# Third mixer of a two-block transformer: where the compression products stand between the projections

## What is computed

```python
def mixer_c(x, w_in, gate_b, cmp_pos, cmp_w1, cmp_w2, w_out, rel_bias):
    p = jnp.einsum('bsd,de->bse', x, w_in)
    q = p[..., :1024] ...
    kv = p[..., C_OFF_KV:C_OFF_GATE].reshape(Bn, S, 3, 2, G, E)
    gates = jax.nn.sigmoid(p[..., C_OFF_GATE:] + gate_b)
    def compress(t, pos, w1, w2):
        blocks = t[:, cidx] + pos[None, None, :, None, :]
        flat = blocks.transpose(0, 3, 1, 2, 4).reshape(Bn, G, n_cmp, CMP_BLOCK * E)
        return jax.nn.gelu(flat @ w1) @ w2
    k_cmp = compress(kv[:, :, 0, 0], cmp_pos[0], cmp_w1[0], cmp_w2[0])
    v_cmp = compress(kv[:, :, 0, 1], cmp_pos[1], cmp_w1[1], cmp_w2[1])
    ...
    # three attention branches per head: compressed, selected, window
    return jnp.einsum('bse,ed->bsd', g0 * o_c + g1 * o_s + g2 * o_w, w_out)
```

## Time and profile before

| | before |
|---|---|
| median of 3 runs | 2474.19 us (2473.15 to 2478.47) |
| the profiled execution, its own time | 2479.86 us |
| its span from first to last instruction | 2478.1 us |
| mean granted TensorE clock | 0.965 |
| busy: PE / DVE / ACT / POOL | 2356.3 / 1589.9 / 1010.6 / 81.4 us |
| mixer `c`, from the first product of c_in.1 to the first score on VectorE | 1930.90 to 1997.11 us |

### The profile page before, as it was taken

How to read it: one execution, slowest core, us unless ns; L and a number is a source line. 1 busy time by engine, 2 the same in 40 slices (tenths; PEclk the granted TensorE clock), 3 DMA queues, 4 the chain that set the end, 5 groups by cost and what they waited for, 6 DMA issues and landing times.

```text
span 2478.1 us, 41302 instructions
## 1 busy us (share of the span) xinstructions
PE 2356.3 (95%) x17730; PEld 2051.0 (83%) x17730; DVE 1589.9 (64%) x2291; ACT 1010.6 (41%) x1327; POOL 81.4 (3%) x116
## 2 busy tenths in 40 slices
PE   6999989999999998889999999999999979999997
PEld 6999749999999777787999988777787958777786
DVE  7887476876887636654755674533796465543795
ACT  3333254334333132342334552433674352433673
POOL 0000000000000002550000000000000000000000
PEclk8999989999999999999999998999999988999999
DMA  8986304874777231001754530867993520877991
GB/s 332 356 314 250 127 26 159 300 286 148 287 302 293 98 136 52 3 3 60 264 179 179 165 101 1 337 271 275 366 353 140 204 91 1 332 271 280 362 353 49
DMA packets 48429, 502.13 MB, mean 203 GB/s; under 512 B 4984, under 2 KB 9592, under 8 KB 11000
## 3 DMA queue, kind: packets, MB, share of 16 engines
q1 hardware_dynamic: 42624, 491.57, 52.2%
q10 hardware_dynamic: 5624, 7.93, 1.3%
HBM read 496.33 MB, written 3.15 MB: 202 GB/s over the span
## 4 chain that ended last, share of the span: by engine, by line
PE 78%; DVE 13%; DMA 4%; issue 3%; ACT 2%; POOL 1%; DVEq 0%; SPq 0%; ACTq 0%; POOLq 0%
PE PS L629 23%; PE PS L1273 21%; PE PS L699 7%; PE PS L675 5%; DMA ring<-stream 4%; PE PS L1284 2%; PE PS L576 2%; DVE work L1975 2%; PE PS L1300 1%; PE PS L1008 1%; PE PS L712 1%; PE PS L811 1%; DVE w_up_lo L2016 1%; DVE work L2188 1%; PE PS L1359 1%
## 5 line engine op out<-in xcount | busy, mean ns | idle before, releaser
L629 PE MATMUL PS<-x_part_hi,w_up_hi 128*128 128x256 f32 x1408 | 404.4, 287 | 11.4 <-DVE w_up_lo L2016 7.7
L629 PE MATMUL PS<-x_part_hi,w_up_lo 128*128 128x256 f32 x1408 | 398.4, 283 | 0.0
L629 PE MATMUL PS<-x_part_lo,w_up_hi 128*128 128x256 f32 x1408 | 398.4, 283 | 0.0
L2591 DVE TENSOR_TENSOR ring_low<-ring,m_w_up 128x2048 fp32r<-128x2048 f32 x96 | 219.6, 2291 | 144.6 <-ACT m_w_up L1814 144.6
L629 PEld LDWEIGHTS PS<-x_part_hi,w_up_hi 128*128 128x128 f32 x1408 | 269.8, 192 | 16.1 <-DVE w_up_lo L2016 10.1
L629 PEld LDWEIGHTS PS<-x_part_lo,w_up_hi 128*128 128x128 f32 x1408 | 270.2, 192 | 0.0
L629 PEld LDWEIGHTS PS<-x_part_hi,w_up_lo 128*128 128x128 f32 x1408 | 270.0, 192 | 0.0
L1814 ACT ACTIVATE m_w_up<-ring 128x2048 fp32r<-128x2048 f32 x96 | 183.9, 1916 | 150.9 <-PE PS L1273 137.1
L2016 DVE TENSOR_TENSOR w_up_lo<-ring,w_up_hi 128x2048 fp32r<-128x2048 f32 x88 | 201.2, 2289 | 20.0 <-ACT w_up_hi L1471 20.0
L1273 PE MATMUL PS<-ring_low,xg_hi 128*128 128x512 f32 x512 | 202.8, 396 | 0.0
L1273 PE MATMUL PS<-m_w_up,xg_lo 128*128 128x512 f32 x512 | 202.2, 395 | 0.0
(11 more groups left out here) (533 smaller groups left out, 4939.8 us busy)
## 6 DMA issues: line engine op xcount, KB each, us to landing
ring<-stream SPq DMA_DIRECT2D x133, 2048.0 KB, 7.9
ring<-stream SPq DMA_DIRECT2D x88, 1536.0 KB, 6.8
work<-stream SPq DMA_DIRECT2D x48, 1024.0 KB, 7.8
hT<-stream SPq DMA_DIRECT2D x16, 1024.0 KB, 9.1
ring<-stream SPq DMA_DIRECT2D x3, 1152.0 KB, 5.7
const<-const_tables ACTq DMA_DIRECT2D x1, 2207.0 KB, 12.4
bias_scratch<-work ACTq DMA_DIRECT2D x1, 2048.0 KB
work<-bias_scratch ACTq DMA_DIRECT2D x2, 1024.0 KB, 6.9
```

What stands on the lines that cost most here:

```text
L629: last = mm(out, w[a][:, lo:lo + P], x[b][:, at:at + T], start=start and i == 0, stop=stop and i == 2, skip_group_check=skip)
L2591: tt_(ring_low[n][:, part], ring[n][:, part], m_w_up[g % 3][:, :].bitcast(F32), ALU.subtract).then_inc(S("up_split"), 1)
```

## The change

The columns of `w_in` are packed in another order: c_in.0 is now the source of the compression, c_in.1 and c_in.2 are the queries, c_in.3 and c_in.4 keys and values as before. In the load list two compression pieces stand behind c_in.1, two behind c_in.2, and `cmp_w2` behind c_in.3. TensorE does the first two compression pieces behind c_in.1, the other two behind c_in.2, the sum over groups between the two halves of c_in.3, the second product ahead of c_in.4. ScalarE and VectorE follow this order, the results go to other PSUM banks (6, 7 for the compression, 0 to 3 for keys and values), and ScalarE's roundings keep their place ahead of the copies.

```diff
@@ stream_plan
-    p += c_in[:1] + [("c_gates", 8 * 24)] + c_in[1:]
-    p += [("cmp_w1.0", 4096), ("cmp_w1.1", 4096), ("cmp_w1.2", 4096), ("cmp_w1.3", 4096), ("cmp_w2", 512)]
+    cmp_w1 = cols("cmp_w1", [512] * 4)
+    p += c_in[:1] + [("c_gates", 8 * 24), c_in[1]] + cmp_w1[:2] + [c_in[2]] + cmp_w1[2:] + [c_in[3], ("cmp_w2", 512), c_in[4]]
@@ TensorE, c()
-                for i, b in ((3, 6), (4, 0)):
-                    pe.wait_ge(S("c_copied"), 2)
-                    g = HALF_AT[f"c_in.{i}"]
-                    half_tiles(g, mix_x, [2 * b, 2 * b + 1])
-                    half_tokens(g + 1, mix_x, lambda tt: bank(b + 1, T, tt * T))
-                pe.wait_ge(S("c_copied"), 5)
-                line.next("cmpb_ready")
-                for kv in range(2):
+                def compress(kv):
...
+                for i in range(3):
+                    split_piece(f"c_in.{i}", mix_x, range(4 * i, 4 * i + 4), passes=None if i else x_halves())
+                    if i == 0:
+                        take("c_gates")
+                        by_token("c_gates", 6, 0, 24, 24, 24, ("c_gate_b", 0)).then_inc(slot_free, 1)
+                    else:
+                        if i == 1:
+                            pe.wait_ge(S("c_copied"), 2)
+                            line.next("cmpb_ready")
+                        compress(i - 1)
+                pe.wait_ge(S("c_copied"), 1)
+                g = HALF_AT["c_in.3"]
+                half_tiles(g, mix_x, [0, 1])
+                pe.wait_ge(S("c_copied"), 4)
                 for kv in range(2):
                     line.next("cmp_raw")
...
                 last.then_inc(S("cmp_turned"), 1)
+                half_tokens(g + 1, mix_x, lambda tt: bank(1, T, tt * T))
                 take("cmp_w2")
...
                 last.then_inc(slot_free, 1)
+                g = HALF_AT["c_in.4"]
+                half_tiles(g, mix_x, [4, 5])
+                half_tokens(g + 1, mix_x, lambda tt: bank(3, T, tt * T))
                 pe.wait_ge(S("cmp_copied"), 1)
                 pe.wait_ge(S("c_copied"), 6)
                 attention("c")
@@ ScalarE, c()
-                for i, (dst, b) in enumerate(((W(C_Q, 1024), 0), (W(C_Q + 1024, 1024), 2), (W(C_SRC, 1024), 4))):
+                for i, (dst, b) in enumerate(((W(C_SRC, 1024), 0), (W(C_Q, 1024), 2), (W(C_Q + 1024, 1024), 4))):
                     mix_highs("c", 2 * i + 3, 2 * i + 4)
                     act.wait_ge(*used(f"c_in.{i}"))
...
-                mix_highs("c", 9)
-                for i, b in ((3, 6), (4, 0)):
-                    act.wait_ge(*used(f"c_in.{i}"))
-                    fn(W(C_KV + 512 * (i - 3), 512), bank(b), ACT.Copy)
-                    fn(W(C_KV + 1024 + 512 * (i - 3), 512), bank(b + 1), ACT.Copy).then_inc(S("c_copied"), 1)
...
-                mix_highs("c", 10)
+                mix_highs("c", 9)
                 act.wait_ge(slot_free, FREED["cmp_w2"])
...
+                for i, b in ((3, 0), (4, 2)):
+                    act.wait_ge(*used(f"c_in.{i}"))
+                    fn(W(C_KV + 512 * (i - 3), 512), bank(b), ACT.Copy)
+                    fn(W(C_KV + 1024 + 512 * (i - 3), 512), bank(b + 1), ACT.Copy).then_inc(S("c_copied"), 1)
+                    if i == 3:
+                        mix_highs("c", 10)
@@ VectorE, c()
-                mix_lows("c", 2, 3, 4, 5, 6, 7, 8)
-                dve.wait_ge(S("c_copied"), 4)
+                mix_lows("c", 2, 3, 4)
+                dve.wait_ge(S("c_copied"), 1)
...
-                mix_lows("c", 9)
+                mix_lows("c", 5, 6, 7, 8, 9)
                 dve.wait_ge(S("bias_in"), 64)
@@ packing of the weights
-    put_cols("c_in", w[:, :2560])
+    put_cols("c_in", np.concatenate([w[:, 1024:1536], w[:, :1024], w[:, 1536:2560]], 1))
```

More of the change, by code:

```diff
@@ L1406, in c @@
                             n = 32 if at + 32 <= 960 else 2 * NCMP
-                            last = mm(bank(4 + 2 * kv, T, T, lo, lo + n), b3[:, at:at + n],
+                            last = mm(bank(6 + kv, T, T, lo, lo + n), b3[:, at:at + n],
                                       piece(name)[:, i * T:(i + 1) * T], start=(half == 0 and i < 4),
@@ L1421, in c @@
                 for m in range(2):
-                    mm(bank(3, 2 * NCMP), w2[:, m, :], hid[:, m, :], start=(m == 0), stop=(m == 1))
+                    mm(bank(7, 2 * NCMP), w2[:, m, :], hid[:, m, :], start=(m == 0), stop=(m == 1))
                 for g in range(2):
                     for m in range(2):
-                        last = mm(bank(3, P, P + g * P, 0, NCMP), hid[:, 2 + m, g * NCMP:(g + 1) * NCMP], w2[:, 2 + m, :],
+                        last = mm(bank(7, P, P + g * P, 0, NCMP), hid[:, 2 + m, g * NCMP:(g + 1) * NCMP], w2[:, 2 + m, :],
                                   start=(m == 0), stop=(m == 1))
                 last.then_inc(slot_free, 1)
+                g = HALF_AT["c_in.4"]
+                half_tiles(g, mix_x, [4, 5])
+                half_tokens(g + 1, mix_x, lambda tt: bank(3, T, tt * T))
                 pe.wait_ge(S("cmp_copied"), 1)
@@ L1912, in c @@
                         fn(W(C_G, 48), bank(6, 48), ACT.Sigmoid).then_inc(S("c_copied"), 1)
-                mix_highs("c", 9)
-                for i, b in ((3, 6), (4, 0)):
-                    act.wait_ge(*used(f"c_in.{i}"))
-                    fn(W(C_KV + 512 * (i - 3), 512), bank(b), ACT.Copy)
-                    fn(W(C_KV + 1024 + 512 * (i - 3), 512), bank(b + 1), ACT.Copy).then_inc(S("c_copied"), 1)
                 for kv in range(2):
                     act.wait_ge(slot_free, FREED[f"cmp_w1.{2 * kv + 1}"])
-                    fn(W(C_RAW + kv * T, T), bank(4 + 2 * kv, T, T), ACT.Copy).then_inc(S("cmp_raw"), 1)
+                    fn(W(C_RAW + kv * T, T), bank(6 + kv, T, T), ACT.Copy).then_inc(S("cmp_raw"), 1)
                 act.wait_ge(S("cmp_turned"), 1)
@@ L1924, in c @@
                 last.then_inc(S("hid_gelu"), 1)
-                mix_highs("c", 10)
+                mix_highs("c", 9)
                 act.wait_ge(slot_free, FREED["cmp_w2"])
-                fn(W(C_KC, 30), bank(3, 30), ACT.Copy)
-                fn(W(C_VC, 256, 0, NCMP), bank(3, 256, P, 0, NCMP), ACT.Copy).then_inc(S("cmp_copied"), 1)
+                fn(W(C_KC, 30), bank(7, 30), ACT.Copy)
+                fn(W(C_VC, 256, 0, NCMP), bank(7, 256, P, 0, NCMP), ACT.Copy).then_inc(S("cmp_copied"), 1)
+                for i, b in ((3, 0), (4, 2)):
[4 more added lines that the diff above has]
+                        mix_highs("c", 10)
                 attention("c", {6: [lambda: mix_highs("c", 11)]})
```

## The result

Beside five runs of each, the change took 2488.31 us (median, 2481.95 to 2493.03) and the kernel before 2477.56 us (2473.15 to 2482.93). The ratio is 1.0037, with a 95% interval of 1.0020 to 1.0055: **slower**, by 5 to 14 us; that is under one per cent, but the interval lies clear of 1. Measured again later, with 12 runs (median 2486.77 us) beside 35 of the kernel before (median 2480.05 us, 2472.60 to 2487.51), the ratio is 1.0026 (1.0012 to 1.0040), or 6.4 us.

What follows compares the result with a forecast made beforehand. The prediction took a chain 78% TensorE and 13% VectorE as the bound. Terms up to the first score gave +5.0 us, with +1.8 for the clock and -1.25 for attention +5.5; 2474.19 + 5.5 = 2479.7 us, range 2475.3 to 2483.5.

Steps and rivals of the forecast that it cites:

- The step that failed: Carrying the difference from the profiled execution, 2479.86 us, to the runs' median, 5.7 us lower: 2474.19 + 5.5 = 2479.7 us.
- rival C: Clock low throughout: both compression pieces at half, attention no better, 3.6 us more at half; +10.3, 2484.5 us; chance 0.08.
- first two pieces: The first two compression pieces on TensorE, one at full and one at half clock: 5.4 us, bounds 3.6 and 7.2.
- half 7 with the clock's loss: Half 7 behind the small products: 5.67 us, plus 1.8 us for half clock after the wait, bounds 0 and 1.8.
- copies and subtraction at the end: Behind c_in.4's last product: copies 1.1 us, then VectorE's subtraction for half 10, 2.2 us, before the first score.
- First stall: Before the first compression product: ScalarE holds the source's copy behind half 4's rounding, waiting for c_in.2's load; TensorE stands 5.0 us.
- Second stall: Before half 6: c_in.3 lands 5.75 us behind cmp_w1.3, and its split takes 4.25 us; TensorE waits 1.1 us.
- Rival B: Loads come faster, 4.83 us behind another instead of 5.75, second stall vanishes: +2.6, 2476.8 us, nothing measurable; chance 0.11.
- Third stall: Before the raw results' products: ScalarE's copies stand behind half 8's rounding, which waits for c_in.4's load; TensorE waits 2.5 us.
- The second product: The product between half 7 and c_in.4, taken from the earlier timeline (1992.02 to 1994.06): 2.04 us.
- Attention: Behind the block: attention starts behind dense work, so less half clock; 1.25 us taken back, bounds 0 and 3.0.
- A: ScalarE is not held and the three stalls do not arise: -6.7, 2467.5 us, faster; chance 0.07.

Runs made afterwards that it cites:

- b1: The change with ScalarE copying the compression's source before half 4's rounding and VectorE adding positions before half 4's subtraction; block 67.7 us, whole 1.0000 against the kernel before.
- c1: The change with only its load list altered, c_in.2 loaded fourth again, ahead of the four compression pieces; block 75.7 us, whole 1.0033 against the kernel before.
- b2: The change with ScalarE copying c_in.2's result and the two raw results before half 8's rounding; block 66.9 us, whole 1.0005 against the kernel before.
- b3: The change with both ScalarE reorderings, those of b1 and b2; block 67.5 us, whole 0.9997 against the kernel before.
- e1: The change with VectorE's subtraction of half 10 moved ahead of its wait for the sixth c_copied count; block 71.0 us, whole 1.0017 against the kernel before.
- e2: The change with the edits of b2 and e1 together; block 66.1 us, whole 1.0004 against the kernel before.
- a0: The change run again without an edit; block 72.6 us, whole 1.0026 against the kernel before.
- v1: Another order than the change's: two compression pieces behind c_in.2, two behind c_in.4, loads and helper lists re-sorted; block 60.0 us, whole 0.9957 against the kernel before.
- v2: The kernel of v1 run again without an edit; block 59.9 us, whole 0.9977 against the kernel before.

## Why the prediction was right or wrong

The direction was right and so were two of the three stalls; the absolute time and its range were wrong: 2479.7 us with 2475.3 to 2483.5, against 2488.31 us. In microseconds against before the forecast was +5.5, the first comparison gave +9.2 (5 to 14), the second +6.4 (3.0 to 9.9).

**The step that failed** is the one that carried the difference to the median of the runs: "2474.19 + 5.5". The three runs behind 2474.19 covered 5 us. Thirty-five runs of the same kernel cover 15 us and have their median at 2480.05. I knew from the page that the profiled execution lay 5.7 us higher, took that as an offset, and gave the base no width at all; the range held only unknowns of the change. Against a base of 2480 the sum ends at 2485.5 us, 1 us from the 2486.77 us of the repeated measurement. Of the first comparison the base explains a part only. Its own base, the median of five, was 2477.56 us; from there the sum ends at 2483.1 us and its range at 2486.9, still under 2488.31. Of the 8.6 us missed, 3.4 are this base, and 5.2 are a difference of medians of 10.75 us where I had 5.5. That the same two kernels lay 6.7 us apart in the repeated measurement suggests that most of the 5.2 us is the scatter of five runs, and not an error of the sum. Besides, the prediction's "2475.7 to 2483.2" is printed without its working, and it is not what its bounds give: those add up to +0.1 and +8.6, and +10.3 is reached only with the extra 1.8 us of rival C.

Term by term, against the first trace of the change:

| term | forecast | measured |
|---|---|---|
| wait before the first compression product | 5.0 | 5.24 |
| first two pieces | 5.4 | 5.21 |
| c_in.2 | 11.34 | 11.56 (1959.18 to 1970.74) |
| last two pieces | 3.6 | 3.63 |
| wait before half 6 | 1.1 | 0 |
| wait before the raw sums | 2.5 | 3.34 |
| half 7 with the clock's loss | 5.67 + 1.8 | 7.27 (1984.52 to 1991.79) |
| second product | 2.04 | 1.43 (1991.79 to 1993.22) |
| c_in.4 | 11.34 | 11.71 (1993.22 to 2004.93) |
| copies and subtraction at the end | 3.3 | 3.4 (2004.93 to 2008.34) |
| block against before, ahead of attention | +6.8 | +6.47 |
| attention, first score to last | -1.25 | +0.2, and -0.9 in the repeated trace |

That +6.8 and +6.47 lie so close is in part luck: the wait before half 6 and the second product came out 1.7 us too high in the forecast, the wait before the raw sums and the projections c_in.2 and c_in.4 1.4 us too low.

*First stall*: right in place, cause and size; b1 and c1 show that it is half 4's place on ScalarE and c_in.2's place in the ring, for either edit removes it.

*Second stall*: wrong, and its size went into the third. I had loads land 5.75 us behind one another. The pair in the place of the earlier trace rows lands 5.9 us apart (issued 1931.52 and 1935.76, 7.8 and 9.5 us), but cmp_w1.3 and c_in.3 (issued 1957.58 and 1959.31) only 4.9:

```profile
ring<-stream SPq DMA_DIRECT2D x1, 2048.0 KB, 7.5
ring<-stream SPq DMA_DIRECT2D x1, 2048.0 KB, 10.7
```

The Trainium skill's page "DMA: Bandwidth & Descriptors", section "Anatomy of one DMA", gives its fit (2.0 us and the bytes at 436 GB/s) for DMAs issued by GpSimd, and these loads are issued by SyncE, which the prediction does not say. As an estimate for 2048 KB the fit makes 4.8 us behind another load and 6.8 us alone. Here one of the two pairs agrees with it (4.9 us) and the other does not (5.9 us), and a load alone took 7.6 us (c_in.4, issued 1972.74). Rival B was right about that one pair, not about the time, since TensorE, starting half 6 earlier, waited 0.8 us more behind it.

*Third stall and its clock*: right. b2 took the wait and the half clock out together, and the block fell by 5.7 us.

*The second product* was read from a stretch partly at half clock: the prediction has 1.00 everywhere but in the rows it names, yet the granted clock was 0.50 from 1993 us on. Behind dense work it took 1.4 us. A gain of 0.6 us missed.

*Attention*: in the change's first trace the gain taken back is not there, for the clock fell to 0.50 with the first score. The other traces speak for it. In b1, b2, b3, e1 and e2, whose attention stands behind the same dense work, the clock stayed at 1.00 for another 5 us, and attention took 50.9 to 52.3 us against the 52.9 of the one trace before; in a0 and c1 it fell at once, and attention took 52.0 and 52.1. Behind small products (v1, v2) it took 53.0. So the -1.25 us may be right on the average; one trace before can't decide it, and what makes the clock fall at once or later is open. The first score and two microseconds further, in the change and in b1 (columns as in the earlier trace rows):

```profile
2008.34:2010.34 2.00, 1.28 (x4) 0.97 (x5) 1.76 (x8) 0.75 (x5) 0.00 (x0) 0.52 0.00 0
2010.34:2012.34 2.00, 1.04 (x5) 0.93 (x4) 1.42 (x5) 1.21 (x5) 0.00 (x0) 0.50 0.00 0
```
```profile
2002.86:2004.86 2.00, 0.96 (x5) 0.56 (x5) 1.83 (x9) 0.75 (x5) 0.00 (x0) 1.00 0.00 0
2004.86:2006.86 2.00, 0.58 (x4) 0.48 (x4) 1.83 (x8) 1.75 (x8) 0.00 (x0) 1.00 0.00 0
```

*The rivals*: A would have needed c_in.2's landing by 1935.2; in the change it landed at 1945.3 with everything 4.8 us later, so within half a microsecond of the time foreseen. C, the clock low throughout, did not come. The measured range of the whole reaches up to C's +10.3, the block does not.

## What to carry to other kernels

In a strict list with a ring of load slots, moving a piece moves its load, and every instruction behind the first that waits for that load. Before laying work between tiles, write down for each load which slot it waits for and when it lands, and sort the helper engines' lists by those landings; the same idea, the compression between the projections, gained 6 us in the block or lost 6, by where it was put and how the loads and lists followed. And give the base of a prediction the width that repeated measurements of unchanged code have: single runs of the kernel before lay 15 us apart, and its medians, of 3 to 35 runs, between 2474.2 and 2480.3 us, as far apart as the effect.

## What the runs showed that I had not expected

Equal code reached the start of c_in.1 anywhere between 1927.5 and 1938.9 us in twelve traces, 11.4 us apart, and took 476.0 to 481.4 us behind the block. The granted clock goes with this behind the block: from the first score to the end it was 0.98 in the three traces with 476.0 us (b1, b2, e1), 0.97 in e2 with 478.2, and 0.96 in the eight others, with 478.2 to 481.4. Whether it makes all of the scatter, and what decides how often it falls in equal code, I did not find out. Inside the block of the change's two traces it does not vary so: the stretch at half clock around the first compression pieces stands at the same place, 17 to 22 us behind the start of c_in.1 (1953 to 1957 in one, 1948 to 1952 in the other, which runs 5 us earlier).

How long TensorE stays at 0.50 behind a wait differs. Behind 4.4 us of waiting, the split products of half 6 ran at 0.50 until about 1977 (b1, b3), 6 us from their first; behind 5.2 us the compression pieces were back at full clock 3 us from their first, and so was half 7, split products again, behind 3.3 us of waiting (0.76 at 1987 to 1989, then 1.00). So neither the length of the wait nor the kind of product by itself orders these three cases, and the reason is open.
